# Second half of the prompt's projection moved from the first phase into slots of the fused phase; keys and values stored straight to the outputs

## The reference

```
p = rms_norm(x) @ w_in              # 1024 -> 2304 columns, 18 blocks of 128
q_sb, k_sb, v_sb, q_sw, k_sw, v_sw = split(p)   # 512, 512, 512, 512, 128, 128
o_sb = stick_breaking(q_sb, k_sb, v_sb)         # causal, 8 heads; the sample also sees 2048 cached keys
o_sw = window_attention(q_sw, k_sw, v_sw)       # 64-token chunks, window 128, ALiBi, sinks
h  = x + concat(rms_norm(o_sb), rms_norm(o_sw)) @ w_out
y  = h + peer_ffn(rms_norm(h))                  # 8 heads: top 16 x 16 of 128 + 128 keys, the best 16
                                                # of 16384 experts; gather rows u, v of each (1024 each)
```

## Time and profile before

| what | value |
|---|---|
| median of 3 runs | 3515.25 us (3509.33 to 3540.03) |
| profiled execution | 3522.34 us, its span 3520.7 us |
| busy, share of the span | PE 75%, DVE 63%, POOL 46%, ACT 39% |
| mean over the span | 344 GB/s on the DMA engines |
| first phase | 0 to 354.8 us |
| fused phase up to the first gather | 354.8 to 466.1 us |
| gathers issued | 466.1 to 3490.7 us |

### The profile page before, as it was taken

How to read it: one execution, slowest core, us unless ns; L and a number is a source line. 1 busy time by engine, 2 the same in 40 slices (tenths; PEclk the granted TensorE clock), 3 DMA queues, 4 the chain that set the end, 5 groups by cost and what they waited for, 6 DMA issues and landing times.

```text
span 3520.7 us, 38247 instructions
## 1 busy us (share of the span) xinstructions
PE 2625.7 (75%) x10640; PEld 1198.8 (34%) x10640; DVE 2232.0 (63%) x5639; ACT 1376.9 (39%) x3205; POOL 1633.1 (46%) x1627
## 2 busy tenths in 40 slices
PE   7999567767867876787778777877787777767664
PEld 4544343223322432243234323432343234322221
DVE  2110167667867676677677767777777766675775
ACT  1000225335523642365246524653565344442222
POOL 0010024554555555545654465555454654555453
PEclk9999678889887988898889888998898988888877
DMA  6222159999999999999999999999999999999887
GB/s 229 86 85 73 53 212 352 394 405 388 373 397 396 374 385 408 374 375 384 413 386 391 382 405 367 403 370 403 374 383 375 394 402 378 406 389 399 345 342 300
DMA packets 248992, 1210.25 MB, mean 344 GB/s; under 512 B 28944, under 2 KB 98352, under 8 KB 112592
## 3 DMA queue, kind: packets, MB, share of 16 engines
q0 software_dynamic: 156416, 1122.51, 80.0%
q1 hardware_dynamic: 92368, 85.36, 7.4%
HBM read 1183.98 MB, written 28.38 MB: 344 GB/s over the span
## 4 chain that ended last, share of the span: by engine, by line
PE 32%; DMA 20%; DVE 14%; issue 7%; ACT 6%; POOL 5%; DVEq 3%; ACTq 2%; SPq 1%; POOLq 0%
DMA f_uv<-peer_uv,f_idx 17%; PE f_y_acc L1342 15%; PE f_q_ps L1284 5%; DVE f_uv L890 5%; POOL f_uv L682 4%; PE f_z L1161 2%; PE f_z L1248 2%; ACT f_diag L830 2%; DMA f_work<-cache_sb_kT 2%; POOL f_gate_fold L671 2%; ACT L824 1%; PE f_z L1142 1%; PE f_z L1168 1%; PE f_o_sb L1185 1%; ACTq L828 1%
## 5 line engine op out<-in xcount | busy, mean ns | idle before, releaser
L682 POOL DMA_INDIRECT f_uv<-peer_uv,f_idx x1056 | 1286.7, 1218 | 1519.4 <-PE f_y_acc L1342 1242.5
L890 DVE CUSTOM_DVE_ANT_0 f_uv<-f_uv,f_x_rep 128x1024 f32<-128x1024 f32 x1056 | 1302.6, 1237 | 718.7 <-DMA f_uv<-peer_uv,f_idx 715.2
L1342 PE MATMUL f_y_acc<-f_uv,f_diag 128*64 128x512 f32 x4224 | 1277.1, 727 | 637.4 <-ACT f_diag L830 596.5
L1342 PEld LDWEIGHTS f_y_acc<-f_uv,f_diag 128*64 128x64 f32 x4224 | 305.1, 156 | 1268.7 <-ACT f_diag L830 767.9
L824 ACT ACTIVATE f_act_hid<-f_hid 128x2 f32<-128x2 f32 x528 | 107.3, 203 | 1293.4 <-DVE f_hid L890 1277.1
L1284 PE MATMUL f_q_ps<-w_q,f_xnT 128*128 128x256 f32 x1152 | 315.6, 428 | 62.4 <-DVE f_cut L1009 60.1
L830 ACT ACTIVATE f_diag<-f_gate_fold,f_act_hid 128x64 f32<-128x64 f32 x1056 | 310.0, 340 | 39.7 <-issue 3.1
L671 POOL TENSOR_TENSOR f_gate_fold<-f_fold,f_gates 128x128 f32<-128x128 f32 x528 | 320.9, 608 | 9.6
L1284 PEld LDWEIGHTS f_q_ps<-w_q,f_xnT 128*128 128x128 f32 x1152 | 237.3, 214 | 175.8 <-DVE f_cut L1009 74.7
L285 PE MATMUL proj<-xnT,w_cols 128*128 128x512 f32 (+1 forms) x864 | 283.8, 491 | 2.1 <-DVE nat L253 1.6
L824 ACT ACT_TABLE_LOAD x196 | 251.5, 1283 | 3.5
(11 more groups left out here) (152 smaller groups left out, 2584.2 us busy)
## 6 DMA issues: line engine op xcount, KB each, us to landing
f_uv<-peer_uv,f_idx POOLq DMA_INDIRECT x1056
f_work<-scratch_projT SPq DMA_DIRECT2D x86, 128.0 KB
scratch_projT<-stage POOLq DMA_DIRECT2D x18, 528.0 KB, 3.8
w_cols<-w_in SPq DMA_DIRECT2D x18, 512.0 KB, 3.7
f_work<-scratch_nat SPq DMA_DIRECT2D x72, 128.0 KB
w_q<-w_peer_q SPq DMA_DIRECT2D x1, 8192.0 KB, 25.5
scratch_nat<-nat POOLq DMA_DIRECT2D x10, 512.0 KB, 3.4
x_in<-x_prompt SPq DMA_DIRECT2D x8, 512.0 KB, 3.7
```

Source lines behind the costliest of these rows:

```text
L682: pool.indirect_dma_start(uv[:, n % RING, :], None, io["peer_uv"], bass.IndirectOffsetOnAxis(ap=idx[:, t % 2, head, k:k + 1], axis=0),).th ...
L890: nc.vector.tensor_tensor_reduce(row_u, row_u, x_rep[:, g % 2, :], 1.0, 0.0, ALU.mult, ALU.add, hid[:, n // 2 % 8, n % 2:n % 2 + 1]).then_ ...
L1342: last = nc.tensor.matmul(y_acc[i * GT:(i + 1) * GT, b * 512:(b + 1) * 512], diag[:, batch % 3, i, :], uv[:, n % RING, DM + b * 512:DM + ( ...
```

## The change

The first phase normalises and turns tiles 0 to 3 and the sample first and projects only their 544 tokens: 8 matmuls of 512 and 8 of 32 per column, evacuated by ACT alone. Tiles 4 to 7 are normalised and turned between the first columns and kept (`xnT_late`). Keys and values go from `nat` straight to the outputs, whose rows the attention then reads; of them `projT` keeps only what the attention needs transposed. The constants and keys, before loaded at the start of the fused phase, are loaded here behind x. `w_q` comes in eight pieces of 1 MB, one behind each of columns 4 to 11.

The second half of the prompt (512 tokens) is projected in the fused phase: column i of `LATE_ORDER` (the ten natural ones first) in slots from -91 + 8 i on, one matmul per slot (two in the first), the last at slot 45 + 6. SP loads its `w_in` column (512 KB) when column i - 2 is done, and stores the result. These buffers lie in the memory of `w_out`; so `w_out` is loaded twice, for tile 0 into the gather buffers (`w_first`, 4 MB), and for the rest at slot 54. All columns use one PSUM bank at a time, so column i + 1 waits until ACT's `late_out` has emptied it. Tile 1's attention, tail and routing start 20 slots later (steps at 25 to 37, windows at 47 to 59, tail at 67), its heads are 9 slots apart (95 to 158). The big copies are gone; two small ones stand at the end.

```diff
+EARLY = SEQ // 2
+ORDER = [0, 1, 2, 3, NT, 4, 5, 6, 7]
+N_EARLY = 5
+COLUMNS = SEQ - EARLY
+KEPT = [c for c in range(C_END) if not C_KV + 4 <= c < C_QSW and c != C_END - 1]
+NATURAL = [c for c in range(C_END) if C_KV <= c < C_QSW or c >= C_KVSW]
...
+    r.w_q = sb("w_q", [P, DK, PH * 2 * QH])
+    r.w_out = sb("w_out", [P, DK, DM])
...
+    late = r.w_out[:].rearrange("p k n -> p (k n)")
+    r.xnT_late = late[:, 0:DK * COLUMNS].rearrange("p (k t) -> p k t", k=DK)
+    at = DK * COLUMNS
+    r.w_late = late[:, at:at + 2 * DK * P].rearrange("p (s k n) -> p s k n", s=2, k=DK)
+    at += 2 * DK * P
+    r.stage_late = late[:, at:at + 2 * COLUMNS].rearrange("p (s t) -> p s t", s=2)
+    at += 2 * COLUMNS
+    r.nat_late = late[:, at:at + 2 * COLUMNS].rearrange("p (s t n) -> p s t n", s=2, n=P)
...
+            for i in range(4):
+                load_x(i)
...
+            for c in range(2, C_END):
+                sp.wait_ge(s_mm, c - 1)
+                load_w(c)
+                if 4 <= c < 4 + DK:
+                    sp.dma_start(r.w_q[:, c - 4, :], io["w_peer_q"][(c - 4) * P:(c - 3) * P, :]).then_inc(r.s_w_q, 16)
+            sp.wait_ge(s_late_const, 13 * 16)
...
+            def project(c):
+                pe.wait_ge(s_w[c % 2], (c // 2 + 1) * 16)
+                if c >= 2:
+                    pe.wait_ge(s_ev, c - 1)
+                for a, b in ((0, EARLY), (EARLY, EARLY + TS)):
                     for k in range(DK):
-                        last = nc.tensor.matmul(acc[s][:, a:b], w[:, s, k, :], xnT[:, k, a:b],
+                        last = nc.tensor.matmul(acc[c % 2][:, a:b], w[:, c % 2, k, :], xnT[:, k, a:b],
                                                 start=(k == 0), stop=(k == DK - 1))
                 last.then_inc(s_mm, 1)
...
+            for i in range(N_EARLY):
+                turn_x(i)
+            pe.wait_ge(s_xnT, N_EARLY)
+            for c in range(C_END + 1):
+                if c < C_END:
+                    project(c)
+                if c == 0:
+                    pe.wait_ge(s_late_const, 13 * 16)
+                    for f in range(2):
+                        last = nc.tensor.transpose(turn_s[:, f * NKEY:(f + 1) * NKEY], keys_in[:, f * QH:(f + 1) * QH],
+                                                   ident[:])
+                    last.then_inc(s_keys, 1)
+                if c < len(ORDER) - N_EARLY:
+                    turn_x(N_EARLY + c)
+                if c - 1 in NATURAL:
+                    turn_natural(NATURAL.index(c - 1))
...
-        return 75 + 12 * head
+        return 95 + 9 * head
...
+LATE_ORDER = NATURAL + [c for c in range(C_END) if c not in NATURAL]
+LATE_SLOT = [FIRST_SLOT + 8 * (i + 1) for i in range(C_END)]
+LATE_AT = {slot: i for i, slot in enumerate(LATE_SLOT)}
...
+        w_first = uv[:, 0:4, :].rearrange("p r (k n) -> p (r k) n", n=DM)
...
+        def late_place(i):
+
+            if LATE_SLOT[i] + 8 < -2:
+                return "y_acc"
+            return "o_sb" if LATE_SLOT[i] + 7 < step_slot(1, 0) + 8 else "o_sw"
...
+                if t == SEQ // P - COLUMNS // P:
+                    for s in range(2):
+                        hold(sync, S_LST[s], stage_stores(C_END + s) * 16)
+                        hold(sync, S_LNS[s], nat_stores(len(NATURAL) + s) * 16)
...
+            copies = ((flat(io, "swa_k_sample")[0:WIN - TS, :], io["cache_swa_k"][TS:WIN, :]),
+                      (flat(io, "swa_v_sample")[0:WIN - TS, :], io["cache_swa_v"][TS:WIN, :]))
+
+            def load_late(i):
+                if i >= 2:
+                    hold(sync, S["late_mm"], i - 1)
+                c = LATE_ORDER[i]
+                src = io["w_in"].rearrange("(k p) n -> p k n", p=P)[:, :, c * P:(c + 1) * P]
+                sync.dma_start(r.w_late[:, i % 2, :, :], src).then_inc(S_WL[i % 2], 16)
...
+            def store_late(i):
+                c = LATE_ORDER[i]
+                hold(sync, S["late_ev"], i + 1)
+                sync.dma_start(io["projT"][c, :, EARLY:SEQ], r.stage_late[:, i % 2, :]).then_inc(S_LST[i % 2], 16)
...
-                if 8 <= n < 8 + 2 * len(copies) and n % 2 == 0:
-                    dst, src = copies[n // 2 - 4]
-                    sync.dma_start(dst, src).then_inc(S["copies"], 16)
-            sync.wait_ge(S["copies"], 160)
+                if n == FIRST_SLOT + 3:
+                    load_late(0)
+                    load_late(1)
+                if (i := LATE_AT.get(n - 8)) is not None:
+                    if i + 2 < C_END:
+                        load_late(i + 2)
+                    if LATE_ORDER[i] in KEPT:
+                        store_late(i)
+                if (i := LATE_AT.get(n - 12)) is not None and i < len(NATURAL):
+                    store_late_natural(i)
+                if n == tail_slot(0) - 30:
+                    load_w_out(w_first, "w_first")
+                if n == LATE_SLOT[-1] + 9:
+                    for s in range(2):
+                        hold(sync, S_LST[s], stage_stores(C_END + s) * 16)
+                        hold(sync, S_LNS[s], nat_stores(len(NATURAL) + s) * 16)
+                    load_w_out(w_out, "w_out")
+            for dst, src in copies:
+                sync.dma_start(dst, src).then_inc(S["copies"], 16)
+            sync.wait_ge(S["copies"], 32)
...
+            hold(pool, S["op"], 1)
...
+            def late_out(i):
+                c = LATE_ORDER[i]
+                act.wait_ge(S["late_mm"], i + 1)
+                if stage_stores(i):
+                    act.wait_ge(S_LST[i % 2], stage_stores(i) * 16)
+                if i >= 2:
+                    act.wait_ge(S["late_turned"], min(i - 1, len(NATURAL)))
+                nc.scalar.activation(r.stage_late[:, i % 2, :], late_bank(i), ACT.Copy,
+                                     scale=column_scale(c)).then_inc(S["late_ev"], 1)
...
+                if (i := LATE_AT.get(n - 7)) is not None:
+                    late_out(i)
...
+                if (i := LATE_AT.get(n - 10)) is not None and i < len(NATURAL):
+                    late_natural(i)
...
+            def late_project(i, k):
+                if k == 0:
+                    pe.wait_ge(S_WL[i % 2], (i // 2 + 1) * 16)
+                    if i:
+                        pe.wait_ge(S["late_ev"], i)
+                    if late_place(i) == "o_sb":
+                        pe.wait_ge(S["mA"], 1)
+                    elif late_place(i) == "o_sw":
+                        pe.wait_ge(S["x_rep"], sum(slot < LATE_SLOT[i] for slot in X_AT))
+                last = nc.tensor.matmul(late_bank(i), r.w_late[:, i % 2, k, :], r.xnT_late[:, k, :],
+                                        start=(k == 0), stop=(k == DK - 1), skip_group_check=True)
+                if k == DK - 1:
+                    last.then_inc(S["late_mm"], 1)
+
+            def late_turn(i):
+                pe.wait_ge(S["late_ev"], i + 1)
+                if i:
+                    pe.wait_ge(S["late_nat"], i)
+                for t in range(COLUMNS // P):
+                    last = nc.tensor.transpose(y_acc[:, 512 + t * P:512 + (t + 1) * P],
+                                               r.stage_late[:, i % 2, t * P:(t + 1) * P], ident[:])
+                last.then_inc(S["late_turned"], 1)
...
+                for k in range(DK):
+                    if (i := LATE_AT.get(n - k * 7 // 8)) is not None:
+                        late_project(i, k)
+                if (i := LATE_AT.get(n - 9)) is not None and i < len(NATURAL):
+                    late_turn(i)
```

More of the change, by code:

```diff
@@ L97, in projection_phase @@
+def projection_phase(nc, io, r):
     with ExitStack() as ctx:
@@ L189, in _ @@
             act.preload_act_table_set("natural_log_exp_and_others")
-            def square(t, s, turn, rows):
-                act.wait_ge(s_x[s], (turn + 1) * 16)
-                nc.scalar.activation(squares[0:rows, s % 2, :], x_in[0:rows, s, :], ACT.Square,
+            for i in range(len(ORDER)):
+                rows, s = rows_of(i), i % 4
+                act.wait_ge(s_x[s], (i // 4 + 1) * 16)
+                nc.scalar.activation(squares[0:rows, i % 2, :], x_in[0:rows, s, :], ACT.Square,
@@ L211, in _ @@
-            columns(act, [evacuate])
+                act.wait_ge(s_st[c % 2], kept_before(c) * 32)
+                turned = sum(b < c - 1 for b in NATURAL)
+                if turned:
+                    act.wait_ge(s_tr, turned)
+                nc.scalar.activation(stage[:, c % 2, 0:EARLY], acc[c % 2][:, 0:EARLY], ACT.Copy, scale=column_scale(c))
+                nc.scalar.activation(stage[:, c % 2, EARLY:], acc[c % 2][:, EARLY:EARLY + TS], ACT.Copy,
+                                     scale=column_scale(c)).then_inc(s_ev, 1)
@@ L299, in _, with turn_natural @@
-            columns(pe, [project, turn_natural])
+            def turn_natural(j):
+                c = NATURAL[j]
+                pe.wait_ge(s_ev, c + 1)
+                if j:
+                    pe.wait_ge(s_nat, j)
+                else:
```

(4 more changed lines are left out.)

461 lines of the change are left out of this document (236 added, 225 removed).

## The result

The changed kernel takes 3424.97 us in the median of four runs (3417.69 to 3431.02) against 3515.07 for the kernel before beside it: a ratio of 0.9735, 95% interval 0.9689 to 0.9782, so 90 us less. Predicted was 3438, in 3394 to 3490. The profiled execution of after took 3431.02 us with a span of 3429.2, 91.5 less than before's span of 3520.7.

The account below looks back on a forecast made before the run. The prediction took a 466 us start with hardly any gathers, then 3025 us bound by gather traffic. Span 3520.7 - 123 + 45 + 1 = 3444, given as 3438 for the median, range 3394 to 3490.

Parts of the forecast that it names:

- First phase: Projection before the fused phase: first column at 26.7 us, 8.7 per column, last at 198, fused phase at 208.
- The 16 x 0.43 + 1.75 rule: First phase: a column without eight wide matmuls takes 8.7 us instead of 15.5, saving 123 us over eighteen.
- Up to the first gather: Fused phase before gathers: 127 us from PE's start at 216, so first gather at 343 instead of 466, -123 us.
- margin of 9 us for waits and start: Before the first gather: 2.5 us slow start, 5 for ten single-bank waits, 2 from PE's `select` to POOL.
- The late columns in the gathers' time: Beside the first gathers: each column load takes 32.2 us against 26.8 in eight slots, +38 us for seven.
- first rival: Gathers' time: the queue does not hold the columns up, +7 to +10 instead, total 3400; chance 0.2.
- Tile 1's heads: Tile 1's routing at 9 slots a head instead of 12: not priced, since the sample's heads have that spacing.
- `w_out` again: Second load, 4.2 MB at slot 54 with DMA share near 1: +11 us, less 4 for copies gone.
- the gathers' time: Stretch in which gathers run: late columns and second `w_out` load together cost +45 us, within 0 to +130.
- the end: End of the kernel: two small copies added, +1 us.
- slower rival: Slots -13 to 53: the row-paced queue decides, 170 us in all, total 3563; chance 0.05.
- second rival: Gathers' time: columns cost twice the shortfall, tile 1's k loads caught behind them, +35 us, total 3473; chance 0.17.

Follow-up runs that it names:

- e8: The changed kernel with late columns 0 to 9, those ahead of the first gather, doing one of eight matmuls: 3407.0 us, ratio 0.9674.
- e10: The changed kernel with the loads of late columns 10 to 17 each split into four transfers, 4096 rows of the same bytes: 3429.83 us, ratio 0.974.
- e3: The changed kernel without the second load of `w_out` and PE's wait for it: 3417.01 us, ratio 0.9719.
- e7: The kernel before with a head's chain from queries to `cut` tightened (2, 3, 4, 5, 7 slots instead of 3, 4, 6, 7, 9): 3470.68 us, ratio 0.987.

## Why the prediction was right or wrong

**First phase: right.** The first column and four of the later evacuations (answering to the earlier trace rows), and the fused phase's start (to the earlier trace rows):

```profile
27.71 2.93 PE L354 MATMUL proj<-xnT,w_cols 128*128 128x512 f32 x3 [4.87 <-DVE xnT L318]
...
149.22 0.60 ACT L284 ACTIVATE stage<-proj 128x512 f32<-128x512 f32 x1 [8.47 <-PE proj L354]
...
158.38 0.60 ACT L284 ACTIVATE stage<-proj 128x512 f32<-128x512 f32 x1 [8.47 <-PE proj L354]
...
184.34 0.60 ACT L284 ACTIVATE stage<-proj 128x512 f32<-128x512 f32 x1 [7.97 <-PE proj L354]
...
192.99 0.60 ACT L284 ACTIVATE stage<-proj 128x512 f32<-128x512 f32 x1 [7.97 <-PE proj L354]
...
203.84 0.95 POOL L797 MEMSET f_q_pad<- 128x1024 f32 x1 [5.95 <-POOLq L168]
...
208.20 1.09 SPq L721 DMA_DIRECT2D r_w_out<-w_in  x2
...
212.59 3.48 PE L1401 MATMUL f_y_acc<-r_w_out 128*128 128x512 f32 x4 [17.21 <-DMA r_w_out<-w_in]
```

Forecast were 26.7, a column every 8.7 us, the last at 198, the phase at 208 and the first late matmul at 216. Measured: 27.7; 8.65 between plain columns and 9.15 between those with a turn; 193.0; 203.8; 212.6. The loads kept up. The 16 x 0.43 + 1.75 rule from one row carried the largest term of the sum to within 6 us: 165 from the first column's start to the last evacuation, forecast 171.

**Up to the first gather: right.** 124 us, forecast 127, with PE busy 117.2 against a sum of 118. The margin of 9 us for waits and start was nearly right: PE idled 6.8, of it 3.9 in five waits on the single bank (5 us in ten predicted) and 1.9 for `cut`. That the old waits are covered is shown by e8, in which they come back. The first gather gained 129.6, not 123; half of the difference came before the first late matmul (212.6 for 216) and half in this stretch.

**The late columns in the gathers' time: wrong, +3 instead of +38.** The step that failed is the division in the earlier trace rows: one chain of loads that took 28.6 us from first issue to last landing was divided by its 1024 rows, and the quotient multiplied by the rows of a column: 32.2 us where eight slots give 26.8. Measured were 14.4, and no wait at the late line. SP had spread those issues over 9.7 us, and the last of them alone took 18.4; a landing time that hardly changes with size or rows (14.4 to 17.5 us in after, 14.5 to 16.6 in e10) can't be divided into a rate, and at 14.4 us two buffers of lead covered it. The first rival (chance 0.2) had this part right, and its 190 us for the first 55 gathers stands against 187.5. The Trainium skill, "DMA: Bandwidth & Descriptors", section "Queues, rings and completion order", says that a DMA engine drains a packet of typically 9 to 17 descriptors from one queue before it turns to the next; from this the prediction made a landing of a few microseconds. The trace agrees in direction (14.4 us), but that was too little, and no run here shows how many rows an engine takes at a turn.

**Tile 1's heads: wrong, +24.7 instead of nothing.** The step was "not priced: the sample's heads have that spacing already". That the spacing stands elsewhere says nothing of its cost: the sample's seven waits for `cut` sum to 34.0 us in the trace of before (2800 us on), tile 1's six in after to 22.1, and I had read this very wait in the earlier trace rows, as something that late matmuls would cover. They do not in tile 1's routing, where no late column is left.

**`w_out` again: right** (+7.3 between gathers 55 and 70, +9.4 by e3; forecast +11 less 4). **The sum:** forecast -123 + 45 + 1 = -77, measured -91.5 in the span: the start 6.6 better, the gathers' time +40 instead of +45, by other terms, the end -2 instead of +1. That the measured 3424.97 lies only 13 us from the forecast is in part luck: 35 us too many for the late columns in the first 55 gathers stand against 25 for tile 1's heads that weren't charged. The slower rival (a queue paced by rows) is refuted by e10: even with four times the rows PE waited for less than a microsecond at the late line. The second rival's way, loads caught behind the columns' on SP, did not show in after, but e10's 8.8 us look like it.

## What to carry to other kernels

In a kernel whose engines each run a fixed order, look for the engine that waits for an instruction which stands one place too late in another's list: here one number, 9 changed to 8, gave 60 us, two thirds as much as the whole rearrangement. In the stretches where it stood, 58 us of that wait stood for 51 us of time; in e7's first 55 gathers 16 us of it stood for 2.5, since another wait took its place. When a change alters a spacing, price it by the waits that the same spacing shows elsewhere in the trace. And don't turn the landing time of a small transfer beside heavy traffic into a rate: compare two sizes first.

## What the hardware showed that I had not expected

Under the gathers (8 KB rows, DMA share 0.90) transfers of 64, 256 and 512 KB on the other queue landed in 17.5, 15.2 and 14.4 us (one, one and three transfers), when 512 KB without gathers took 3.9, by the issues of after's first phase:

```profile
w_cols<-w_in SPq DMA_DIRECT2D x18, 512.0 KB, 3.9
```

Four times the rows, of 128 bytes, made that landing about 2 us longer at most, but SP was held at the issue itself, up to 14 us for four transfers. And PE's granted clock was 0.99 of 2.4 GHz in the stretch in which PE was busy 117 of 124 us, and 0.80 in e8's, 73 of 103.
